# Two more chunks of each up projection computed as pairs, and a new order of the products inside every pair

## What is computed

```python
hn = rmsnorm(x, norm_ffn_pre[l])
u = jnp.square(jax.nn.relu(jnp.einsum('bsd,df->bsf', hn, w_up[l])))
y = jnp.einsum('bsf,fd->bsd', u, w_down[l])
x = x + rmsnorm(y, norm_ffn_post[l])
```

## Time and profile before

| | us |
|---|---|
| median of 3 runs | 2559.22 |
| lowest, highest | 2558.97, 2559.31 |
| the profiled execution | 2559.44 |
| its span, first to last instruction | 2557.7 |
| TensorE matmul busy in the span | 2551.5 (100%) |
| TensorE weight load | 2115.1 (83%) |
| VectorE | 1764.6 (69%) |
| ScalarE | 1296.9 (51%) |
| GpSimd | 34.8 (1%) |
| mean granted TensorE clock | 1.000 |

### The profile page before, as it was taken

How to read it: one execution, slowest core, us unless ns; L and a number is a source line. 1 busy time by engine, 2 the same in 40 slices (tenths; PEclk the granted TensorE clock), 3 DMA queues, 4 the chain that set the end, 5 groups by cost and what they waited for, 6 DMA issues and landing times.

```text
span 2557.7 us, 29454 instructions
## 1 busy us (share of the span) xinstructions
PE 2551.5 (100%) x11425; PEld 2115.1 (83%) x11425; DVE 1764.6 (69%) x2062; ACT 1296.9 (51%) x1554; POOL 34.8 (1%) x56
## 2 busy tenths in 40 slices
PE   9999999999999999999999999999999999999999
PEld 7888888888888888888888888888888888888887
DVE  5646565566666666776876777678678768778686
ACT  6554443444555555455454544445465455455463
POOL 1000000000000000000000000000020000000000
PEclk9999999999999999999999999999999999999999
DMA  8767766676776777778566787666757677666674
GB/s 271 216 189 210 205 202 196 190 208 204 215 220 196 215 196 200 219 227 230 165 181 181 206 223 201 203 206 198 244 174 223 195 216 212 215 196 224 204 231 141
DMA packets 534795, 527.42 MB, mean 206 GB/s; under 512 B 294896, under 2 KB 297824, under 8 KB 534656
## 3 DMA queue, kind: packets, MB, share of 16 engines
q1 hardware_dynamic: 531856, 518.09, 68.3%
q0 software_dynamic: 2384, 6.93, 1.1%
q10 hardware_dynamic: 416, 0.52, 0.1%
HBM read 488.24 MB, written 2.10 MB: 192 GB/s over the span
## 4 chain that ended last, share of the span: by engine, by line
PE 100%; ACT 0%; DVE 0%; issue 0%; ACTq 0%
PE bank L2312 30%; PE bank L2313 30%; PE bank L2314 30%; PE bank L2379 2%; PE bank L2380 2%; PE bank L2381 2%; PE bank L2498 1%; PE bank L2487 1%; PE bank L2477 1%; PE bank L2411 0%; PE bank L2420 0%; PE bank L2433 0%; PE bank L2426 0%; PE bank L2558 0%; PE bank L2545 0%; PE bank L2578 0%
## 5 line engine op out<-in xcount | busy, mean ns | idle before, releaser
L1255 DVE TENSOR_TENSOR t_wl<-t_stage,t_wh 128x1024 fp32r<-128x1024 f32 x844 | 1021.4, 1220 | 600.2 <-ACT t_wh L714 594.8
L714 ACT ACTIVATE t_wh<-t_stage 128x1024 fp32r<-128x1024 f32 x845 | 885.1, 1057 | 801.4 <-PE bank L2314 758.3
L2312 PE MATMUL bank<-t_wl,t_xth 128*128 128x512 f32 x2400 | 941.0, 392 | 0.5 <-DVE t_xtl L1297 0.5
L2314 PE MATMUL bank<-t_wh,t_xtl 128*128 128x512 f32 x2400 | 934.1, 389 | 0.0
L2313 PE MATMUL bank<-t_wh,t_xth 128*128 128x512 f32 x2400 | 934.0, 389 | 0.0
L2314 PEld LDWEIGHTS bank<-t_wh,t_xtl 128*128 128x128 f32 x2400 | 450.5, 188 | 94.1
L2312 PEld LDWEIGHTS bank<-t_wl,t_xth 128*128 128x128 f32 x2400 | 450.6, 188 | 93.9 <-DVE t_xtl L1297 0.9
L2313 PEld LDWEIGHTS bank<-t_wh,t_xth 128*128 128x128 f32 x2400 | 450.7, 188 | 92.5 <-issue 0.2
L2312 PE MATMUL bank<-t_wl,t_yth 128*128 128x512 f32 x914 | 355.6, 389 | 0.0
L2313 PE MATMUL bank<-t_wh,t_yth 128*128 128x512 f32 x914 | 355.1, 389 | 0.0
L2314 PE MATMUL bank<-t_wh,t_ytl 128*128 128x512 f32 x914 | 355.1, 389 | 0.0
(11 more groups left out here) (410 smaller groups left out, 1509.4 us busy)
## 6 DMA issues: line engine op xcount, KB each, us to landing
t_stage<-in_a_w_in_dram SPq DMA_DIRECT2D x192, 512.0 KB, 4.3
t_stage<-in_w_in_dram SPq DMA_DIRECT2D x168, 512.0 KB, 4.3
t_stage<-in_b_w_in_dram SPq DMA_DIRECT2D x128, 512.0 KB, 4.5
t_stage<-in_w_up_dram SPq DMA_DIRECT2D x92, 512.0 KB, 4.4
t_stage<-in_w_down_dram SPq DMA_DIRECT2D x90, 512.0 KB, 5.1
t_stage<-in_a_w_out_dram SPq DMA_DIRECT2D x64, 512.0 KB, 4.3
t_ubuf<-in_w_down_dram SPq DMA_DIRECT2D x38, 512.0 KB, 5.3
t_ubuf<-in_w_up_dram SPq DMA_DIRECT2D x36, 512.0 KB, 4.5
```

What stands on the lines that cost most here:

```text
L714: e.activation(wh[:, j % N_SPLIT], stage[s], ACT.Copy).then_inc(*hi(j))
L1255: e.tensor_tensor(low, src, high.bitcast(F32), ALU.subtract).then_inc(*lo(j))
L2312: e.matmul(o, h, w_l, start=start, stop=False)
L2314: return e.matmul(o, l, w_h, start=False, stop=stop)
```

## The change

In `halved_pairs`, (up,q,2) with (up,q,3) become pairs for all four q; only (up,0,0), (up,0,1) and the last two down chunks stay plain in the feed-forward network. In `groups_of`, P2, P3 and P4 of every pair (the ones in the other stages too) stand behind the first, second and third round of one group of a and one of b. `low_after` gets new values. ScalarE's and VectorE's lists are written anew: sum, relu, square, transposition of both chunks of a pair come ahead of the low parts of both, and the combinations of the next pair's banks stand between. In q = 0 the token sums of the up projection are made behind chunk 0 and no longer behind chunk 1. GpSimd's first load of the last norm's row waits for P3 of (up,3,2).

```diff
--- before.py
+++ after.py
@@ -128,7 +128,7 @@
 
     return ([(("gm", c), ("ga", c)) for c in (2, 3)] +
             [(("w_out", 0), ("w_out", 1))] +
-            [((kind, q, c), (kind, q, c + 1)) for q in range(4) for kind, c in (("up", 0), ("down", 0), ("down", 2))
+            [((kind, q, c), (kind, q, c + 1)) for q in range(4) for kind in ("up", "down") for c in (0, 2)
              if (kind, q, c) not in (("up", 0, 0), ("down", 3, 2))])
 
 
@@ -249,8 +249,7 @@
         a, b = pairs[m]
         own = []
         for n, k in enumerate((4, 6, 8, 10)):
-            own += [(a, k)] + {0: [(m, P2)], 1: [(m, P4)]}.get(n, [])
-            own += [(b, k)] + ([(m, P3)] if n == 0 else [])
+            own += [(a, k), (b, k)] + {0: [(m, P2)], 1: [(m, P3)], 2: [(m, P4)]}.get(n, [])
         return own + [(a, 12), (a, 14), (b, 12), (b, 14)]
 
     units = []
@@ -289,9 +288,8 @@
 
     def low_after(q, c):
 
-        if ("up", q, c) in pair_of:
-            return 8 if c == 0 else 10
-        return 8 if c == 3 else 4
+        behind = 4 if q == 0 and c < 2 else (6, 10, 4, 8)[c]
+        return behind + end("up", q, c if q == 0 and c < 2 else c | 1) - end("up", q, c)
 
     def when(n):
         return same_time[n]
@@ -693,7 +691,7 @@
                 e.tensor_tensor(h, h, d, ALU.add).then_inc(*pool("x3", c, i))
 
         for c in range(4):
-            e.wait_ge(*(vec.at("dr", c - 2, 1) if c >= 2 else used.at(where[first_of["up", 3, 0], P3])))
+            e.wait_ge(*(vec.at("dr", c - 2, 1) if c >= 2 else used.at(where[first_of["up", 3, 2], P3])))
             load_row(c, A["norm_ffn_post_2"][:, cols(c)], "ffn", c)
 
 
@@ -1176,37 +1174,38 @@
                 sum_high("up", q)
 
         e.wait_ge(*vec.at("sF"))
+        def squared(q, c):
+
+            t = buf[c % 2]
+            slot(end("up", q, c))
+            if ("up", q, c) in pair_of:
+                e.wait_ge(*vec.at("sum", "up", q, c))
+            else:
+                e.wait_ge(*used.at(end("up", q, c) - 1))
+            for i in range(2):
+                e.activation(t[:, i, :], t[:, i, :] if ("up", q, c) in pair_of else accs("up", q, c)[i],
+                             ACT.Relu, scale=sF[:, i:i + 1]).then_inc(*act("up", q, c, i))
+            e.wait_ge(*act.at("up", q, c, 1))
+            e.activation(t, t, ACT.Square).then_inc(*act("squared", q, c))
+
         for q in range(4):
-            for c in range(4):
-                if (q, c) == (0, 2):
-                    slot(end("up", 0, 1) + 2)
-                    sum_high("x3")
-                early_turn = ("up", q, 1) in pair_of
-                if c == 3 and early_turn:
-                    up_high(q, 1)
-                if c and not (c == 1 and early_turn):
-                    up_high(q, 0 if c == 2 and early_turn else c - 1)
-                if c == 3:
-                    m = first_of["down", q, 0]
-                    apart(m, vec.at("late", m - 2, 1) if q >= 2 else None)
-                slot(end("up", q, c))
-                halved_ = ("up", q, c) in pair_of
-                if halved_:
-                    e.wait_ge(*vec.at("sum", "up", q, c))
-                else:
-                    e.wait_ge(*used.at(end("up", q, c) - 1))
-                    if (q, c) >= (0, 2):
-                        e.wait_ge(*turned.at("up", *((q, c - 2) if c >= 2 else (q - 1, c + 2))))
-                for i in range(2):
-                    e.activation(buf[c % 2][:, i, :], buf[c % 2][:, i, :] if halved_ else accs("up", q, c)[i],
-                                 ACT.Relu, scale=sF[:, i:i + 1]).then_inc(*act("up", q, c, i))
-                e.wait_ge(*act.at("up", q, c, 1))
-                e.activation(buf[c % 2], buf[c % 2], ACT.Square).then_inc(*act("squared", q, c))
+            squared(q, 0)
+            if q == 0:
+                slot(end("up", 0, 0) + 3)
+                sum_high("x3")
+                up_high(0, 0)
+            squared(q, 1)
+            apart(first_of["up", q, 2], turned.at("up", q, 0))
+            if q:
+                up_high(q, 0)
+            up_high(q, 1)
+            squared(q, 2)
+            squared(q, 3)
+            apart(first_of["down", q, 0], vec.at("late", first_of["down", q - 1, 2], 1) if q >= 2 else None)
+            up_high(q, 2)
             up_high(q, 3)
-            if ("down", q, 2) in first_of:
-                m = first_of["down", q, 2]
-                apart(m, vec.at("late", m - 1, 1) if q else None)
-            if ("up", q + 1, 0) in first_of:
+            if q < 3:
+                apart(first_of["down", q, 2], vec.at("late", first_of["down", q, 0], 1) if q else None)
                 apart(first_of["up", q + 1, 0], turned.at("up", q, 2))
 
 
@@ -2140,29 +2139,31 @@
                     e.tensor_tensor(buf[c][:, i, :], d, rowb[:, c % 2, :], ALU.mult).then_inc(*vec("dr", c, i))
 
         for q in range(4):
-            if ("up", q, 0) in pair_of:
+            if q:
                 for c in range(2):
                     up_sum(q, c)
                     up_turn(q, c)
+            else:
+                up_turn(0, 0)
+                slot(end("up", 0, 0) + 2)
+                split_sums(xth, xtl, rowb.rearrange("p a b -> p (a b)"), vreg[:, 7168:8192], "x3")
+                slot(end("up", 0, 0) + 3)
+                sum_low("x3")
+                up_low(0, 0)
+                up_turn(0, 1)
+            slot(end("up", q, 1) + 2)
+            together(first_of["up", q, 2], turned.at("up", q, 1))
+            if q:
                 up_low(q, 0)
-            else:
-                up_turn(q, 0)
-                up_low(q, 0)
-                slot(end("up", 0, 1))
-                split_sums(xth, xtl, rowb.rearrange("p a b -> p (a b)"), vreg[:, 7168:8192], "x3")
-                up_turn(q, 1)
-                slot(end("up", 0, 1) + 3)
-                sum_low("x3")
-                up_low(q, 1)
-            up_turn(q, 2)
-            if ("up", q, 0) in pair_of:
-                up_low(q, 1)
-            up_low(q, 2)
+            up_low(q, 1)
+            for c in (2, 3):
+                up_sum(q, c)
+                up_turn(q, c)
             if q:
                 late(first_of["down", q, 0])
             else:
                 together(first_of["down", q, 0])
-            up_turn(q, 3)
+            up_low(q, 2)
             up_low(q, 3)
             down_evac(q, 0)
             down_evac(q, 1)
```

## The result

Four runs gave a median of 2617.69 us (2614.57 to 2619.88), against 2559.26 us for the kernel before (2558.97 to 2559.42); ratio 1.0228, 95% interval 1.021 to 1.0245. The change is 58.4 us slower where 51.0 was forecast; the time lies in the stated range. The profiled execution took 2619.88 us with a span of 2618.1, 60.4 us more than the one of before.

What follows compares the result with a forecast made beforehand. TensorE was taken as the bound, at 0.2266 us per matmul. Waits at the new borders of 56.4 us less 5.4 for 24 fewer matmuls gave +51.0, so 2610.2 us, range 2585 to 2624.

Steps and rivals of the forecast that it cites:

- chain of the second sum: Border behind an up pair: VectorE's second sum ends at 13.9 us, TensorE wants its banks at 10.9, so waits 3.0.
- P3's and chunk 2's low parts: Borders up to down: TensorE waits 1.5 + 3 x 4.0 us for P3's low part, 4 x 2.0 for chunk 2's.
- The moved products and loads at nothing: Every pair: spreading P2, P3, P4 over three rounds gains 0; loads and the moved GpSimd wait cost 0.
- Unknown: the clock: TensorE's clock behind mid-stage waits: taken at 0, upper bound 19 us from half-rate groups behind seven long waits.
- signs of being wrong: TensorE running through each new pair's second group, waits standing at loads, or a clock below 1.00 behind the waits.
- the low parts behind the combinations: New borders: TensorE waits 3 x 1.2 us up to up, and 1.5 + 3 x 4.0 us for P3 up to down.
- the second sums of q = 1 to 3: Borders up to down: VectorE is 1.7 us late, so TensorE's wait for the sum is 4.7 us each.
- The clock rival: The clock falls behind TensorE's waits, or loads come late as well: 2620 to 2629 us, chance 0.14.
- Only the banks wait: Waits of 3.0 us at 7 borders and 5.2 at the first, later lateness absorbed: 2580; chance 0.14, with cases between.
- Only the matmul count tells: A pair's second sum is written before 10.9 us, so nothing waits: 2553.8 us, chance 0.04.

Runs made afterwards that it cites:

- the kernel with the order alone: Kernel before, with only the new order of P2, P3 and P4 in its 13 pairs and no new pairs: 2559.27 us, ratio 1.0000.
- the dosed ones: Kernel before, with TensorE made to wait for a later low part at one group in each of q = 1 to 3: 2573.17 us.
- the one with early token sums: Kernel after, with only the first up projection's token sums moved ahead of the norm: 2614.52 us.
- a single edit: Kernel after, with the second sum of an up pair behind one low part past the border instead of four: 2591.67 us, ratio 1.0124.
- the reordered kernel: Kernel after, all pairs kept, VectorE's and ScalarE's lists rewritten in order of need, q = 0 ordered like the other q: 2554.51 us, ratio 0.9981.
- the kernel with the old order: Kernel after, with the old order of P2, P3 and P4 inside the pairs: 2622.26 us, ratio 1.0241.

## Why the prediction was right

**The mechanism, point by point.** The chain of the second sum came out as added up from the rows of before: 13.9 us forecast behind the border, and TensorE's wait, 3.0 forecast for four borders, is 3.04 to 3.05 at those four. P3's and chunk 2's low parts were the next late things, in the places named. The moved products and loads at nothing: right, by the kernel with the order alone and by the absence of any wait of TensorE for a load. Moving the second sum alone removed all seven of its waits.

**The terms that were mis-sized.** The step "Unknown: the clock", taken at 0 with an upper bound of 19 us, measured 18.7 in the profiled execution, and 21.9 with P3's slow products: past the bound. My reason, that the nearest rows are all at 1.00, was weak, since none of those rows had a wait of this length in it; and the clock fell at ten places, q = 0's border among them, which the bound had left out. A clock below 1.00 behind the waits was one of my own signs of being wrong, and it came: the time lies in the range although this term was wrong. The Trainium skill's page "TensorE: Matmul & The Clock Gate", in the part on the HAM clock gate, says that an idle engine falls to half rate. Most waits here agree, with 0.57 and 0.50 behind the dosed ones of 3.09 and 4.21 us; the one of 3.07 us in the kernel after was followed by no fall.

Against that, the other terms came out 9.9 us smaller (46.5 for 56.4): 7.9 at the low parts behind the combinations (0 for 3.6 up to up, 9.2 for 13.5 at P3) and 2.2 at the second sums of q = 1 to 3. While TensorE runs slowly behind a wait, VectorE catches up, so part of the clock's cost is taken off the next wait. The borders up to down of q = 1 to 3 show it, in the kernel after and in the one with early token sums. What was lost behind the border before (1.5 to 3.0 us) and the wait for the sum (4.6 to 3.1) add up to 6.0 or 6.1 us at all six; what was lost behind this wait (0.1 to 2.9) and the wait for P3 (4.1 to 1.4) to 4.2 or 4.3. At (down,2,0) of the kernel after VectorE had caught up fully: the wait for the sum was 3.07 and not 4.7, no clock was lost there, and P3's wait was then the longest, 4.1 for the 4.0 forecast. The sum, 18.7 - 9.9 = 8.8, is the distance of the 59.8 found to the 51.0 forecast. That the two errors take each other off in part was not foreseen; the number owes some of its nearness to that.

**The rivals.** The clock rival came true in its mechanism, and the time lies between the forecast and its lower edge (2610, 2617.7, 2620). "Only the banks wait" was wrong, but near what a single edit gives (2591.67). "Only the matmul count tells" is where the reordered kernel ends, 2554.51 for 2553.8: the condition I had set for it, the second sum before 10.9 us, could be met with the same work. Its argument that 0.82 us was enough for 1700 us rests on no row: the 0.82 us were read at one border.

**Spread.** The kernel after ran over 5.3 us from lowest to highest in four runs, before over 0.45. The mean granted clock of the four is 0.990, 0.992, 0.990 and 0.993 for times of 2619.88, 2616.10, 2619.29 and 2614.57 us: the slower runs have the lower clock. That the clock is the whole of the spread is argued, not shown.

## What to carry to other kernels

When an engine works a list in order, ask of each instruction on a new border not how long it is but what stands ahead of it that waits for another engine: here two sums of 0.68 us, behind a transposition that waits for ScalarE, cost 26 us of 2618. Write the instruction that frees another engine's banks at the moment at which it becomes possible, and fill the round trips with work that is due later; the same 24 matmuls saved then gave 4.8 us and not a loss of 58. And price a wait of TensorE of 2 us or more above its length, as a range: behind waits of 2 to 6 us in the kernels here some 1.5 to 3.0 us more were lost in most cases and 0.1 to 0.3 in some. Then ask what is late next, since a loss ahead of it can be taken off that wait.

## What was not expected of the hardware

A single wait of TensorE of 3.09 us in a stream that had run at full clock for over 2 ms was enough for the clock to fall: the clock was granted in full up to the wait's end and 0.57 in the 4 us behind it, 1.7 us lost. 2.8 us were lost behind 4.21 us, where the clock had fallen before the wait ended (0.50 from 2441.5 to 2442.6 us), and 0.2 behind 1.95 us with the clock at 1.00. In the kernel after the loss behind a border's wait for the sum was 1.7 to 3.0 us at six borders, and 0.1 at the seventh, of 3.07 us; in the kernel with the old order 1.8 us were lost behind 2.06. So the length does not tell what a wait costs; what else it depends on was not tried.
